# Long heads: value products over the head's own keys as three products of high and low parts

## The reference, cut to what matters

```
def _diff_attn(qb, k_all, v_all, lam):
    s = einsum('bqhid,bkhid->bhiqk', qb * ATTN_SCALE, k_all)
    p = softmax(s, axis=-1)
    a = p[:, :, 0] - lam * p[:, :, 1]
    return einsum('bhqk,bkhe->bqhe', a, v_all)
```

## Time and profile before

| | us |
|---|---|
| median of three runs | 3295.22 (3292.26 to 3297.37) |
| span of the profiled execution | 3295.4 |
| TensorE busy | 3186.3 (97%) |
| VectorE busy | 2232.1 (68%) |
| ScalarE busy | 1344.1 (41%) |
| GpSimd busy | 293.7 (9%) |
| value products of c, a and b (L1405), sum of their records | 93.4 |

### The profile page before, as it was taken

The page is one execution under the profiler, slowest core; times in us unless marked ns, Lnnn a source line. Parts: engine busy times, 40 slices in busy tenths (PEclk is TensorE's granted clock), DMA queues, the critical chain, the costliest instruction groups (busy, mean ns, idle before and its releaser), DMA issues.

```text
span 3295.4 us, 47837 instructions
## 1 busy us (share of the span) xinstructions
PE 3186.3 (97%) x16736; PEld 2611.4 (79%) x16736; DVE 2232.1 (68%) x3546; ACT 1344.1 (41%) x2059; POOL 293.7 (9%) x521
## 2 busy tenths in 40 slices
PE   5999999999999999999999999999998999999997
PEld 1799989788777777888888777777786888888786
DVE  1677778756777765687655777774677899655446
ACT  1445555323444444236422344444326323454424
POOL 0000011101101100110101000000112000000001
PEclk8999999999999999999999999999999999999999
DMA  9865557565444433664756443432553422222233
GB/s 397 293 223 204 192 208 251 192 217 189 144 156 162 144 122 103 251 214 152 265 185 217 152 154 130 158 130 78 186 205 136 141 92 99 98 86 86 103 115 103
DMA packets 111316, 554.44 MB, mean 168 GB/s; under 512 B 17920, under 2 KB 22064, under 8 KB 68304
## 3 DMA queue, kind: packets, MB, share of 16 engines
q1 hardware_dynamic: 51424, 348.15, 29.8%
q0 software_dynamic: 59760, 204.55, 18.4%
HBM read 530.55 MB, written 22.04 MB: 168 GB/s over the span
## 4 chain that ended last, share of the span: by engine, by line
PE 78%; DVE 9%; DMA 5%; issue 3%; ACT 3%; DVEq 2%; ACTq 0%; POOL 0%; POOLq 0%; SPq 0%
PE acc L1265 23%; PE acc L1267 22%; PE acc L1266 22%; PE pv L1405 2%; DVE w_lo L1737 2%; DMA gates<-in_wm 2%; DMA xy<-in_wm 2%; PE S L1379 2%; PE S L1394 1%; DVE gates L1790 1%; ACT work L688 1%; ACT w_hi L688 1%; DVE small L1904 1%; PE misc L1416 1%; PE acc L1289 0%
## 5 line engine op out<-in xcount | busy, mean ns | idle before, releaser
L1265 PE MATMUL acc<-h_hi,w_hi 128*128 128x512 f32 (+1 forms) x4608 | 1676.5, 364 | 11.7 <-DVE w_lo L1737 7.0
L1267 PE MATMUL acc<-h_hi,w_lo 128*128 128x512 f32 (+1 forms) x4608 | 1646.1, 357 | 0.0
L1266 PE MATMUL acc<-h_lo,w_hi 128*128 128x512 f32 (+1 forms) x4608 | 1644.4, 357 | 0.0
L1265 PEld LDWEIGHTS acc<-h_hi,w_hi 128*128 128x128 f32 x4608 | 870.8, 189 | 165.6 <-issue 30.3
L1266 PEld LDWEIGHTS acc<-h_lo,w_hi 128*128 128x128 f32 x4608 | 871.5, 189 | 127.4 <-issue 6.9
L1267 PEld LDWEIGHTS acc<-h_hi,w_lo 128*128 128x128 f32 x4608 | 870.8, 189 | 127.7
L1737 DVE TENSOR_TENSOR w_lo<-raw,w_hi 128x1024 fp32r<-128x1024 f32 x592 | 698.4, 1221 | 195.0 <-ACT w_hi L688 191.3
L688 ACT ACTIVATE w_hi<-raw 128x1024 fp32r<-128x1024 f32 x592 | 593.5, 1054 | 53.0 <-DMA raw<-in_w 20.4
L688 ACT ACTIVATE ev<-acc 128x512 f32<-128x512 f32 (+1 forms) x210 | 110.8, 532 | 832.4 <-PE acc L1267 810.8
L497 POOL DMA_DIRECT2D gates<-in_wm x288 | 153.3, 532 | 1412.8 <-DVE gates L1790 1224.8
L688 ACT ACTIVATE work<-S,small 128x768 f32<-128x768 f32 (+1 forms) x160 | 129.1, 814 | 259.3 <-DVE small L1904 259.3
(11 more groups left out here) (271 smaller groups left out, 2400.2 us busy)
## 6 DMA issues: line engine op xcount, KB each, us to landing
raw<-in_w SPq DMA_DIRECT2D x296, 1024.0 KB, 5.0
gates<-in_wm POOLq DMA_DIRECT2D x288, 512.0 KB, 4.7
xy<-in_wm SPq DMA_DIRECT2D x32, 1024.0 KB, 8.8
x_d<-xy POOLq DMA_DIRECT2D x1, 4096.0 KB, 15.2
qb<-x_d POOLq DMA_DIRECT2D x16, 256.0 KB, 3.9
kb<-x_d POOLq DMA_DIRECT2D x16, 256.0 KB, 4.2
bias_d<-kb POOLq DMA_DIRECT2D x8, 384.0 KB, 20.5
out_y<-xy SPq DMA_DIRECT2D x3, 1024.0 KB, 4.6
```

The costliest lines, as they stand in the source:

```text
L1265: mm(o, w_hi[:, w], h_hi[:, x], start=n == 0, stop=False)
L1266: mm(o, w_hi[:, w], h_lo[:, x], start=False, stop=False)
L1267: last = mm(o, w_lo[:, w], h_hi[:, x], start=False, stop=n == len(ks) - 1)
```

## The change

The own keys' part of the value product (four of six key blocks) is computed as three F32R products: high values with high map, high values with low map, low values with high map. The context's two key blocks stay F32.

- ScalarE writes the transposed map's own part to `a_hi` (F32R) and the context's part to `a_t` as before: two instructions where there was one. The values go to `v_hi` (F32R).
- VectorE gets `attention_low(i, p)`: `S` less `a_hi` into `a_lo`, once for each of the four query blocks, and `value_low(i)`: the transposed values less `v_hi` into `v_lo`. Blocks 0 to 2 are subtracted at the start of the next p, ahead of `lo`; block 3 at the end of the step, behind `gated`. `value_low` is between maxima and difference of p = 0.
- TensorE waits for `alo_done` ahead of the scores and of the value product, for `vlo_done` ahead of the value product and of the mean squares. The scores of p = 1 to 3 stand ahead of block 4 of the weight tile, not of block 3.
- `a_lo` has the place of tiles 12 to 15 of `xy`, `a_hi` that of the first four blocks of `a_t`, `v_lo` that of `qb`, `v_hi` that of the first 512 columns of `vtok`. VectorE's wait for the store of the context's rows (`x_st`) goes to the start of step 1 of pass a.

```diff
 # ScalarE, attention_evac
-                    f(a_t[:, 0:NK // P * T].rearrange("p (k t) -> p k t", t=T)[:, :, P * p:P * (p + 1)],
-                      S[:, 0:NK].rearrange("p (k q) -> p k q", q=P)).then_inc(at_evac, 1)
+                    f(a_hi3[:, :, q], S[:, 0:SEQ].rearrange("p (k q) -> p k q", q=P))
+                    f(a_t[:, SEQ * SEQ // P:].rearrange("p (k t) -> p k t", t=T)[:, :, q],
+                      S[:, SEQ:NK].rearrange("p (k q) -> p k q", q=P)).then_inc(at_evac, 1)
 # ScalarE, value_evac
-                    f(vtok[:, 0:T], misc[:, 0:T]).then_inc(vt_evac, 1)
+                    f(vtok[:, 0:T] if c == "c" else v_hi[:], misc[:, 0:T]).then_inc(vt_evac, 1)
 # TensorE, scores
                         pe.wait_ge(at_evac, shown(at_evac, n))
+                        pe.wait_ge(alo_done, shown(alo_done, n - 16))
 # TensorE, values
+                        pe.wait_ge(alo_done, shown(alo_done, At(N0[c] - 16, QT, i)))
+                        pe.wait_ge(vlo_done, shown(vlo_done, At(h0 - 8, 1, i)))
+                        for k in range(SEQ // P):
+                            v, a = slice(P * k, P * (k + 1)), slice(k * T, (k + 1) * T)
+                            mm(pv[:, 0:T], v_hi[:, v], a_hi[:, a], start=k == 0, stop=False)
+                            mm(pv[:, 0:T], v_hi[:, v], a_lo[:, a], start=False, stop=False)
+                            mm(pv[:, 0:T], v_lo[:, v], a_hi[:, a], start=False, stop=False)
+                        for k in range(SEQ // P, NK // P):
+                            last = mm(pv[:, 0:T], vtok[:, P * k:P * (k + 1)], a_t[:, k * T:(k + 1) * T],
+                                      start=False, stop=k == NK // P - 1)
 # TensorE, step
-                        weight_tile(..., beside=beside[p] if attn else None)
+                        weight_tile(..., beside=beside[p] if attn else None, beside_n=4 if p else 3)
 # VectorE
+                def attention_low(i, p):
+                    dve.wait_ge(at_evac, shown(at_evac, At(N0[c] - QT + p + 1, QT, i)))
+                    q = slice(P * p, P * (p + 1))
+                    tt(a_lo3[:, :, q], S[:, 0:SEQ].rearrange("p (k q) -> p k q", q=P), a_hi3[:, :, q].bitcast(F32),
+                       ALU.subtract).then_inc(alo_done, 1)
+                def value_low(i):
+                    dve.wait_ge(vt_evac, shown(vt_evac, At(VT0[c], 1, i)))
+                    tt(v_lo[:], misc[:, :], v_hi[:].bitcast(F32), ALU.subtract).then_inc(vlo_done, 1)
 # VectorE, step
+                    if c == "a" and not norm and attn:
+                        dve.wait_ge(x_st, shown(x_st, 16))
                     for p in range(4):
+                        if attn and p > 0:
+                            attention_low(i, p - 1)
                         lo(j_at(phase, i, p) + 1 if proj else j_at(c + "pool", 0, p + 1))
                         if attn:
                             maxima(i, p)
-                        if attn:
+                            if p == 0:
+                                value_low(i)
                             difference(i, p)
...
                     if proj:
-                        if c == "a" and not norm and attn:
-                            dve.wait_ge(x_st, shown(x_st, 16))
                         gated(i)
+                    if attn:
+                        attention_low(i, 3)
```

More of the change, by code:

```diff
@@ L137, in build @@
         h_lo = sb("h_lo", KT * SEQ, F32R)
+        with nc.sbuf_tensor("below_a_lo", [P, 12 * SEQ], F32):
+            with nc.sbuf_tensor("a_lo", [P, 4 * SEQ], F32R) as a_lo:
+                pass
         xy = sb("xy", KT * SEQ)
@@ L144, in build @@
         evt = sb("evt", SEQ)
+        with nc.sbuf_tensor("below_a_hi", [P, 1536], F32):
+            with nc.sbuf_tensor("a_hi", [P, 4 * SEQ], F32R) as a_hi:
+                pass
         work = sb("work", 4608)
+        with nc.sbuf_tensor("v_lo", [P, SEQ], F32R) as v_lo:
+            pass
         qb = sb("qb", SEQ)
@@ L150, in build @@
         qk = sb("qk", 2 * SEQ + 2 * (SEQ + CTX), F32R)
+        with nc.sbuf_tensor("v_hi", [P, SEQ], F32R) as v_hi:
+            pass
         vtok = sb("vtok", 1024)
@@ L189, in build @@
         a_t = work[:, 1536:1536 + 6 * SEQ]
+        a_hi3 = a_hi[:, :].rearrange("p (k t) -> p k t", t=SEQ)
+        a_lo3 = a_lo[:, :].rearrange("p (k t) -> p k t", t=SEQ)
         last_osq = a_t[:, 0:SEQ]
@@ L261, in build @@
         at_evac = sem("at_evac", 4)
+        alo_done = sem("alo_done", 1)
+        vlo_done = sem("vlo_done", 1)
         pv_done = sem("pv_done", 1)
@@ L805, in attention_evac @@
                         act.wait_ge(pv_done, shown(pv_done, At(h0 - 1, 1, i)))
-                    f(a_t[:, 0:NK // P * T].rearrange("p (k t) -> p k t", t=T)[:, :, P * p:P * (p + 1)],
-                      S[:, 0:NK].rearrange("p (k q) -> p k q", q=P)).then_inc(at_evac, 1)
+                    q = slice(P * p, P * (p + 1))
+                    if c == "c":
+                        f(a_t[:, 0:NK // P * T].rearrange("p (k t) -> p k t", t=T)[:, :, q],
+                          S[:, 0:NK].rearrange("p (k q) -> p k q", q=P)).then_inc(at_evac, 1)
+                        return
+                    f(a_hi3[:, :, q], S[:, 0:SEQ].rearrange("p (k q) -> p k q", q=P))
+                    f(a_t[:, SEQ * SEQ // P:].rearrange("p (k t) -> p k t", t=T)[:, :, q],
+                      S[:, SEQ:NK].rearrange("p (k q) -> p k q", q=P)).then_inc(at_evac, 1)
                 def value_evac(i):
                     act.wait_ge(vt_done, shown(vt_done, At(VT0[c] + 1, 1, i)))
-                    f(vtok[:, 0:T], misc[:, 0:T]).then_inc(vt_evac, 1)
+                    f(vtok[:, 0:T] if c == "c" else v_hi[:], misc[:, 0:T]).then_inc(vt_evac, 1)
                 def squared(i, osq):
@@ L1402, in values @@
                     if ctx_keys:
+                        pe.wait_ge(alo_done, shown(alo_done, At(N0[c] - 16, QT, i)))
+                        pe.wait_ge(vlo_done, shown(vlo_done, At(h0 - 8, 1, i)))
                         pe.wait_ge(v_ld, shown(v_ld, At(16 * (h0 - 8), 16, i)))
+                        for k in range(SEQ // P):
[6 more added lines that the diff above has]
+                                      start=False, stop=k == NK // P - 1)
+                        last.then_inc(pv_done, 1)
+                        return
                     for k in range(NK // P):
@@ L1466, in step @@
                         at, n = (phase, i) if proj else (c + "pool", 0)
-                        weight_tile(j_at(at, n, p), a_at(at, n, p), T, H_AT[c + ".h"], beside=beside[p] if attn else None)
+                        weight_tile(j_at(at, n, p), a_at(at, n, p), T, H_AT[c + ".h"], beside=beside[p] if attn else None,
+                                    beside_n=4 if p else 3)
                         if attn:
@@ L2310, in _ @@
             nc.vector.memset(csil0, 0.0)
-            grant(dve, lo_done, hlo_done, sq_added, ssq_added, mod_used, conv_done, qk_ready, gate_used, y_done, r_done, b_used,
+            grant(dve, lo_done, hlo_done, sq_added, ssq_added, mod_used, conv_done, qk_ready, gate_used, y_done, r_done, b_used, alo_done, vlo_done,
                   u2_ready, ypw_done, pool_done, y2_done, gs_done)
```

## The result

The changed kernel takes **3431.39 us** (median; 3430.88 to 3434.35) against 3295.22. The ratio is 1.0414, 95% interval 1.0402 to 1.0425: 4.1% slower. The forecast was 3425 (3392 to 3456), and slower. The profiled execution has a span of 3430.3 us, 134.9 over that of before, and I read the difference from the two spans.

The account below looks back on a forecast made before the run. Matmuls on TensorE, busy 97% of the span, bound the kernel. Per pass 44.8 + 14.4 + 6.6 + 2.0 + 2.0 - 5.5 + 0.8 = 65.1, 130 us in both passes: 3425 us, range 3392 to 3456.

Parts of the forecast that it names:

- The fourth block (a): Value product waits for the subtraction behind the rotary block and gated: 6.4 us, seven times, 44.8 us a pass.
- The first block (b): Tile 1's scores wait for the subtraction behind the third modulation part: 1.1 us in six steps, 6.6 a pass.
- the two steps 1: Step 1 of each pass, without value product: 2.5 us waiting for the first block's subtraction, net +2.0.
- The second block (c): Tile 2's scores wait 0.5 us, net 0.3 a step, 2 us a pass; bounds 0 and 1.2 a step.
- The third: Third block's subtraction, after two modulation parts: costs nothing, at most 0.3 us.
- The clock: TensorE restarts at half speed after a stall: 1.8 us each, eight a pass, 14.4 us; bounds 0 and 2.5 each.
- step 1's wait of 2.5 us: Step 1's stall before the scores, counted as a clock drop too, making eight drops a pass.
- The last head (d): Its value product, already waiting for ScalarE, waits 0.1 us more for ScalarE and 0.7 for VectorE: +0.8 a pass.
- The added work: VectorE grows by 16 x 5 x 0.65 = 52 us of subtractions; ScalarE by about 10 us in all.
- The gain: Value product: four F32 products a head become three F32R each, saving 0.68 us a head, 5.5 a pass.
- the rival's 3286: Fourth block ready before the value product after all, without the first block's waits: 3286 us, chance 0.05.

Follow-up runs that it names:

- x1: Changed kernel with the fourth query block's subtraction moved into the rotary block, ahead of the gate product: 3346.11 us.
- x3: Kernel before, with its F32 value product also waiting for the previous step's gate product in the seven projecting steps a pass, no added work: 3414.01 us.
- x2: Changed kernel with 24 more F32R matmuls ahead of the wait for alo_done in each of the 14 stalled value products: 3406.90 us.
- x4: Changed kernel without low parts and their waits; the three F32R products of a key block all take high parts: 3294.51 us.
- y5: x4 with the value product, value transposes and first scores of tile 0 ahead of weight block 5, not 3: 3294.05 us.

## Why the prediction was right, point by point

- **The fourth block (a)** was right in mechanism, place and number of cases. 6.4 us were forecast and 6.5 measured, up to 6.8. It is shown by x1, which moves this one subtraction, and by x3, which makes the wait alone.
- **The first block (b)**: 1.1 forecast, 0.9 of waiting in the head shown and a distance 1.05 longer. The instructions are those named. VectorE's timeline of the changed kernel:

```profile
1134.10 1.22 DVE L1825 SCALAR_TENSOR_TENSOR gates<-gates 128x1024 f32<-128x1024 f32 x1
...
1139.68 1.23 DVE L1825 SCALAR_TENSOR_TENSOR gates<-gates 128x1024 f32<-128x1024 f32 x1 [3.21 <-DMA gates<-in_wm]
1140.83 0.08 DVE L1825 DVE_READ_ACCUMULATOR gates<-gates 128x1 f32 x1
```

  The third part starts 5.6 us after the first, the subtraction follows it, and the scores start at 1141.57. In the two steps 1, +2.0 was forecast, +2.0 and +1.6 measured.
- **The second block (c)**: 0.3 forecast, 0.5 measured, inside its bounds. The third was free, as said.
- **The clock**: 1.8 a stall was forecast; 2.0 to 2.1 is what the products and the distances show, and 1.75 what x2 gives over all. I had added step 1's wait of 2.5 us to the list of drops; it paid nothing: 9.55 us from its scores to the next transposes, as at full clock. So 16 drops were 14.
- **The last head (d)**: +0.8 forecast. The wait went from 1.2 to 2.3.
- **The added work**, by groups of the changed kernel:

```profile
L1961 DVE TENSOR_TENSOR a_lo<-S,a_hi 128x512 fp32r<-128x512 f32 x64 | 44.0, 687 | 45.6 <-ACT work L702 45.6
...
L1966 DVE TENSOR_TENSOR v_lo<-misc,v_hi 128x512 fp32r<-128x512 f32 x16 | 10.9, 679 | 0.0
```

  80 subtractions of 0.68 to 0.69, 55 us of records; 52 was forecast. ScalarE grew by 5.4 us on the page, where I had said about 10; it is behind no new wait of TensorE.
- **The gain** is the mis-sized term, though not in the sum. Inside the changed kernel the 0.68 a head is there: 6.65 of delay ahead of the product, plus 2.1, less 0.68, is the 8.1 of the table. As I read it, the long stall had given VectorE time in hand; no run tests that by itself. But my sentence "even if everything else were free, the gain is 11 us", and with it the rival's 3286, was wrong as the kernel stood. x4 and y5 made everything else free and gained about 1 us (3294). I had checked that the new waits end late, and not whether the old work, once TensorE comes 0.68 us earlier, is ready: the rotary block had 0.45 us in hand at most, and VectorE's chain to tile 2 about 0.2. The Trainium skill (TensorE: Matmul & The Clock Gate, Architectural detail) calls the queues of ScalarE and VectorE strict FIFO. The runs agree: in x1 the same subtraction, ahead of the gate product and not behind it, took off 85 us.
- **The total** is 6 us off because errors cancel in part: too little by 14 x 0.6 at T3 to T0 and by 12 x 0.2 in the second block, too much by 3.6 for the drops in step 1 that did not come, and within 1 us elsewhere. Without those drops the forecast would have been 3421, 10 us under the result.

## What to carry to other kernels

When a product is split into high and low parts, the low part is a new producer, and its place in its engine's order counts for more than its cost: the same 55 us of subtractions stand in a kernel of 3431 us and in one of 3284. Ask of each wait what stands ahead of the awaited instruction in its own queue, and of each saving which other engine must then be earlier, and by how much it can. If the answer is "by nothing", first move that engine's unwaited work into its idle (here 1.9 us a tile behind the maxima), then make the saving.

## What the runs showed of the hardware that I had not expected

- After a wait of about 2 us TensorE's clock was at half speed only sometimes. In x1 six steps of one pass with waits of 2.0 to 2.4 us took 16.0 or 17.6 to 18.0 us. The wait of 2.53 us in step 1 of the changed kernel had no half speed behind it, nor had those of 2.32 us in its last heads, while in the kernel before an idle of 2.2 us had the earlier trace rows. Behind the waits of 5.6 to 6.8 us, all 14 of them in the changed kernel and in x3, the value product lost time at half speed every time. What decides the short ones is open.
- What a stall costs in clock is not one number. In x3 it was 1.5 to 3.1 us behind nearly equal waits, with a granted clock of 0.77, 0.68 and 0.64 over products of 6.8, 7.7 and 8.2 us; in the changed kernel it was 2.0 on average and varied by 0.6. Whether F32 or F32R products follow is not shown to matter; why x3 varies is open.
- 24 matmuls whose result is thrown away made the kernel faster by 24.5 us (x2), because they kept the granted clock at 1.00.
